# Hybrid encoder step: key caches also laid out token-minor, and attention weights normalised by GpSimd

## The chip, the cores and the metric

The kernel runs on one core of a Trainium2 chip. The metric is device time in microseconds (us) of one execution; three runs of the kernel before are given. The engines are named as the profile names them: PE (TensorE, matrix products and transposes), DVE (VectorE), ACT (ScalarE), POOL (GpSimd), SP (SyncE, which here only issues DMAs).

## The reference

Two layers run over 1024 new frames of one stream (the prompt) and over 16 new frames of each of eight running streams (the samples). The change is in the second layer's attention for the samples. For one sample, with 16 heads and 16 queries each (256 rows), it is

```
def latent_attend(q_lat, q_rope, c, kr, w_uv, mask):
    s = (einsum('bqhk,bsk->bhqs', q_lat, c) + einsum('bqhr,bsr->bhqs', q_rope, kr)) * ATTN_SCALE
    p = softmax(s, axis=-1)
    o_lat = einsum('bhqs,bsk->bqhk', p, c)
    return einsum('bqhk,khv->bqhv', o_lat, w_uv)

c_all  = concatenate([cache_ckv, c_new])      # 1024 past + 16 new rows of 256, per sample
kr_all = concatenate([cache_krope, kr_new])   # the same rows of 64
o = latent_attend(q_lat, q_rope, c_all, kr_all, w_uv, None)
```

The same latent rows `c` are keys (contracted over their 256 features) and values (contracted over the 1040 tokens). The caches arrive token by token, a row of features each.

## The kernel before, in words

The program has five stages, one after the other on the critical engine: mixer A (0 to 583 us of the trace), the middle with the latent keys and the gates (583 to 950), eight head pairs of the prompt's attention (950 to 1573), the eight sample sequences (1573 to about 1726), and the output (to 1943). Each engine's program is written out by hand, and semaphores order them; nothing is scheduled by a planner.

Matrix products are done with both factors split into a rounded high part and a low remainder, three products for each (lines 115 to 117). ACT rounds the high part (`round_high`, line 104), and then DVE subtracts it for the low part (`round_low`, line 109).

For sample i, PE computes `scores(i, 0)` and `scores(i, 1)`, for 128 of the 256 query rows each, and then `values(i - 1)`. Between them it does turns, listed in `TURNS`: W0 to W4 turn the softmax weights `s_p` so that tokens lie on partitions (groups of four 128x128 transposes, W4 of two), and K0 to K6 turn the keys of sequence i + 1 so that features lie on partitions (six groups of four and one of three: 27 transposes for each sequence). The keys of sequence 0 are turned in the last head pair (`turn_first`, from unit `KEYS_FROM` = 9 of its 16 on). Each turned group lands in PSUM; ACT writes its high part (`s_ct_h`, `s_kt_h` for keys, `s_pt_h` for weights), and DVE its low part (`s_ct_l`, `s_kt_l`, `s_pt_l`). Odd and even sequences have their own key buffers.

Softmax on the 128 query rows of one half goes: DVE `largest` (memset of the padding, then the maximum, line 2804), ACT `exp` (line 2669, also sums the rows), DVE `inverted` (reciprocal, line 2808), ACT `normed` (line 2674, scales 128x1056 weights by the reciprocal). `q_low` (line 2737) makes the low parts of the next sequence's queries on DVE, three instructions. SP loads each sequence's cache `s_c_raw`, which is both the values' source and the source of K0 to K3, and the rotary keys `s_kr_raw`.

Of the kernel before, what the change touches and what calls it, by code (L numbers as in the profile page):

```python
# [13 lines left out]
P = 128  # L14
# [988 lines left out]
def middle_programs(nc, k, m, kept_at, heads):  # L1003
# [63 lines left out]
    kvg = late.take("m_kvg", [KVL])  # L1067
    bank = k.bank
# [21 lines left out]
    kv_stored = [m.sem(f"m_kv_stored{i}") for i in range(2)]  # L1090
    (first_high, first_low, wh_ready, wl_ready, gh_ready, gl_ready, y_done, sum_done, stats_done, mv_done, rstd_step,
# [30 lines left out]
    def _(sp):
# [39 lines left out]
        for i in range(NCOL):  # L1162
            if i + 2 < NCOL:
                load_columns(i + 2)
            j = i - 1 - NCQ
            if j >= 0:
                store_gate(j)
                if behind_gate(j)[1] is not None:
                    store_kv(behind_gate(j)[1])
                if j == 8:  # L1170

                    heads.load_first(sp)
                if j == 10:
# [162 lines left out]
    def _(act):  # L1336
# [64 lines left out]
        def turned_high(t):  # L1401
            b, cols = bank[:, 6 + t % 2], slice(t * P, (t + 1) * P)
            act.wait_ge(turned_k, t + 1)
            round_high(nc, k.ct_h[:, :, cols], b[:, 0:2 * P].rearrange("p (a q) -> p a q", a=2))
            round_high(nc, k.kr_h[:, cols], b[:, 2 * P:3 * P]).then_inc(th_k, 1)
# [28 lines left out]
    def _(dve):  # L1434
# [120 lines left out]
        for j in range(HEADS):  # L1555
# [11 lines left out]
            if before is not None:  # L1567
# [7 lines left out]
    def bank_free(pe, b):  # L1575
# [5 lines left out]
        elif b == 6:  # L1581
            pe.wait_ge(c_ready, NT)
# [57 lines left out]
KEYS_FROM = 9  # L1640
NKT = 7
# [16 lines left out]
def heads_programs(nc, k, m, kept_at):  # L1658
# [172 lines left out]
    def _(pe):  # L1831
# [118 lines left out]
        def body(pr, first, last):  # L1950
# [8 lines left out]
            for u in range(UNITS):  # L1959
# [3 lines left out]
                if last and KEYS_FROM <= u < KEYS_FROM + NKT - 1:  # L1963
                    k.samples.turn_first(pe, u - KEYS_FROM)
# [8 lines left out]
            else:  # L1973
                k.samples.turn_first(pe, NKT - 1)
# [313 lines left out]
TURNS = ["W1", "W4", "W2", "W3", "K0", "K1", "K2", "K3", "K4", "K5", "K6", "W0"]  # L2288
BEFORE = TURNS[:4]
# [3 lines left out]
def samples_programs(nc, k, m, kept_at, heads):  # L2293
# [16 lines left out]
    kr_raw = early.take("s_kr_raw", [2, KB + 1, 2, RD])  # L2310
# [9 lines left out]
    block.middle_end = late.regions[0][0]  # L2320
    pt_h, pt_l = late.take("s_pt_h", [KB + 1, QS], F32R), late.take("s_pt_l", [KB + 1, QS], F32R)
# [9 lines left out]
             "o_done o_out ch_ready cl_ready uv_done uv_out og_stored").split()  # L2331
    S = {n: m.sem("s_" + n) for n in names}
    c_loaded = [m.sem(f"s_c_loaded{i}") for i in range(2)]
    kr_loaded = [m.sem(f"s_kr_loaded{i}") for i in range(2)]
    cache_loaded = m.sem("s_cache_loaded")

    def turns(i):

        if not isinstance(i, int):
            return TURNS  # L2340
        return [x for x in TURNS if not (i == 0 and x in BEFORE) and not (i == NSEQ - 1 and x[0] == "K")]

    def turn_number(i, x):

        if isinstance(i, int):
            n = NKT + sum(len(turns(j)) for j in range(i)) + (turns(i).index(x) if i < NSEQ else BEFORE.index(x))
            return n, 6 + n % 2
        at = NKT + len(turns(0)) - len(TURNS) + TURNS.index(x)
        return i * len(TURNS) + at, 6 + at % 2

# [10 lines left out]
    def step_of_keys(j):  # L2361

        return [("c", 0, 0, 4), ("c", 0, 4, 4), ("c", 1, 0, 4), ("c", 1, 4, 4), ("kr", 0, 0, 4), ("kr", 0, 4, 4), ("new", 0, 8, 1)][j]

# [74 lines left out]

    def turn_bank(pe, n, at):  # L2440

        if isinstance(n, int) and n < NKT + 2:
# [4 lines left out]

    def turn_keys(pe, j, b, par):

        what, a, s0, w = step_of_keys(j)  # L2450
        if what == "new":
            for x in range(2):
                nc.tensor.transpose(b[:, x * P:x * P + P], c_raw[par][:, KB, x * P:x * P + P], k.ident[:])
            mm = nc.tensor.transpose(b[:, 2 * P:3 * P], kr_raw[:, par, KB].rearrange("p a b -> p (a b)"), k.ident[:])
        else:
            for x in range(w):
                src = c_raw[par][:, s0 + x, a * P:a * P + P] if what == "c" else kr_raw[:, par, s0 + x].rearrange("p a b -> p (a b)")
                mm = nc.tensor.transpose(b[:, x * P:x * P + P], src, k.ident[:])
        mm.then_inc(S["t_done"], 1)

    def turn_first(pe, j):

        if j == 0:
            heads.bank_free(pe, 1)
            pe.wait_ge(c_loaded[0], 32)
        else:
            pe.wait_ge(S["t_out"], j)
        if j == 4:
            pe.wait_ge(kr_loaded[0], 64)
        turn_keys(pe, j, bank[:, 1], 0)  # L2470

    block.turn_first = turn_first

    @block.tensor
    def _(pe):
# [13 lines left out]
        def turn(x, i, par):  # L2489

            if isinstance(i, int) and i < NSEQ and x not in turns(i):
                return
            n, at = turn_number(i, x)
            if x[0] == "K":

                if x == "K0":
                    pe.wait_ge(c_loaded[1 - par], (i + par) * 16 + 32)
                if x == "K4":
                    pe.wait_ge(kr_loaded[1 - par], (i + par) * 32 + 64)
                turn_keys(pe, int(x[1]), turn_bank(pe, n, at), 1 - par)  # L2500
            else:
                j = int(x[1])
                turn_weights(j, i if j == 0 else i - 1, n, at)

        def scores(i, par, qt, beside):

            q = slice(qt * P, qt * P + P)
            for n, c in enumerate((1, 2, 0) if qt == 0 else (0, 1, 2)):
# [10 lines left out]
                if beside[n]:  # L2519
                    turn(beside[n], i, par)  # L2520

        def values(i, par, beside):


            if isinstance(i, int):
                pe.wait_ge(S["t_out"], turn_number(i + 1, "W3")[0] + 1)
            else:
                pe.wait_ge(S["t_out"], i * len(TURNS) + (turn_number(1, "W3")[0] + 1))
            pe.wait_ge(S["cl_ready"], i * NCP + NCP)
            pe.wait_ge(S["exp_done"], i * 2 + 3 if not (isinstance(i, int) and i == NSEQ - 1) else 2 * NSEQ)  # L2530
            for n in range(6):
# [6 lines left out]
                if beside:  # L2538
                    turn(beside[n], i + 1, 1 - par)

        def body(i, par, first, last):

            pe.wait_ge(S["ql_ready"], i + 1)
            if first:
                for b in range(6):
                    heads.bank_free(pe, b)
                pe.wait_ge(S["t_out"], NKT)
                pe.wait_ge(S["zeroed"], 8)
            else:
                if isinstance(i, int) and i == 1:  # L2550
                    pe.wait_ge(S["zeroed"], 14)
                pe.wait_ge(S["t_out"], turn_number(i, "W1")[0] - 1)

                pe.wait_ge(S["exp_done"], i * 2 - 1)
            if first:

                scores(i, par, 0, ["K0", "K1", "K2"])
                scores(i, par, 1, ["K3", "K4", "K5"])
                for x in ("K6", "W0"):
                    turn(x, i, par)  # L2560
                return
            scores(i, par, 0, ["W1", "W4", "W2"])
# [4 lines left out]
        turn("W1", NSEQ, 0)  # L2567
        k.output.first_columns(pe, 0)
        for x in ("W4", "W2", "W3"):
            turn(x, NSEQ, 0)  # L2570
# [3 lines left out]
        values(NSEQ - 1, 1, None)  # L2574

    def project_values(pe, j):
# [4 lines left out]
        if j < 2:  # L2581
            pe.wait_ge(S["t_out"], turn_number(NSEQ, BEFORE[-1])[0] + 1)
# [50 lines left out]
    def first_keys_high(act, j):  # L2633
        keys_high(act, j, j, 1, 0)
# [627 lines left out]
```

## Time and profile before

| what | value |
|---|---|
| median of three runs | 1944.83 us (1942.0, 1944.83, 1945.01) |
| profiled execution: first to last instruction | 1942.6 us |
| PE busy | 1912.8 us, 98% |
| DVE, ACT, POOL busy | 55%, 39%, 20% |
| first sequence, start to start | 12.84 us |
| a later sequence, start to start | 19.51 to 20.15 us |

The runs list no time apart for the profiled execution; its span lies 2.2 us under the median of the runs. A busy PE means that a product or transpose is in flight. What one sequence costs is read from its start, the first product `ps<-s_ct_h,s_q_l`, to the next sequence's: 1573.30, 1586.14, 1606.29, then every 19.5 to 19.7 us up to 1704.56.

### The profile page before, as it was taken

How to read it: one execution, taken by the hardware profiler on the slowest of the kernel's cores; microseconds unless marked ns; L12 is line 12 of the kernel's file. 1: busy time of each engine (PE TensorE's matmuls, PEld its weight loads, DVE VectorE, ACT ScalarE, POOL GpSimd, SP SyncE). 2: the span in 40 equal slices, each digit the busy share in tenths (PEclk: the TensorE clock that was granted, in tenths of full speed). 3: DMA queues.
4: the chain of work that ended last, by engine and by line, in shares of the span. 5: the costliest groups of instructions: out<-in, count | busy, mean ns of one | idle time of the engine just before them, and what ended most of it. 6: DMA issues, size and time to landing. Idle time of an engine off the chain costs nothing.

```text
span 1942.6 us, 31496 instructions
## 1 busy us (share of the span) xinstructions
PE 1912.8 (98%) x11771; PEld 1807.6 (93%) x11771; DVE 1061.3 (55%) x1943; ACT 767.2 (39%) x1342; POOL 394.0 (20%) x322
## 2 busy tenths in 40 slices
PE   9999999999999999999999999999999999999998
PEld 9999999999987999999999999999999989988886
DVE  4354446445658612332366676666666677653632
ACT  4333233233322222211355555555555567761100
POOL 0221222122311010000042432432433410000000
PEclk9999999999999999999999999999999999999999
DMA  6121122022236312233211112111111253363521
GB/s 183 35 78 54 36 67 78 25 64 68 76 120 201 122 49 70 80 104 106 77 45 50 40 51 64 34 54 54 40 49 42 73 135 93 96 226 136 157 87 44
DMA packets 186082, 158.55 MB, mean 82 GB/s; under 512 B 36144, under 2 KB 170544, under 8 KB 185744
## 3 DMA queue, kind: packets, MB, share of 16 engines
q1 hardware_dynamic: 180784, 139.60, 23.7%
q10 hardware_dynamic: 5040, 17.37, 2.5%
q8 instruction: 58, 0.95, 0.2%
q0 software_dynamic: 176, 0.43, 0.1%
q14 instruction: 24, 0.20, 0.0%
HBM read 115.52 MB, written 41.84 MB: 81 GB/s over the span
## 4 chain that ended last, share of the span: by engine, by line
PE 54%; DVE 7%; issue 5%; ACT 3%; DMA 1%; DVEq 0%; ACTq 0%; SPq 0%
PE ps L115 16%; PE ps L117 16%; PE ps L116 16%; PE ps L1925 1%; PE ps L1908 1%; PE ps L1907 1%; DVE h_pt_l L109 1%; ACT h_p L2042 1%; DVE h_mx L2168 1%; DVE s_mx L2804 1%; DVE h_p L2125 1%; ACT h_p L2031 1%; DVE h_p L2130 1%; DMA m_g_raw<-scratch_o 1%; DVE h_gate L2190 0%
## 5 line engine op out<-in xcount | busy, mean ns | idle before, releaser
L1821 POOL TENSOR_SCALAR h_p<-h_p,h_rsum 128x128 f32<-128x128 f32 (+7 forms) x128 | 220.7, 1726 | 439.8 <-DVE h_rsum L2172 439.8
L115 PE MATMUL ps<-act_h,a_w_l 128*128 128x384 f32 x768 | 270.8, 353 | 1.6 <-DVE a_w_l L109 1.6
L117 PE MATMUL ps<-act_h,a_w_h 128*128 128x384 f32 x768 | 260.1, 339 | 0.0
L116 PE MATMUL ps<-act_l,a_w_h 128*128 128x384 f32 x768 | 259.8, 338 | 0.0
L115 PE MATMUL ps<-act_h,m_c_l 128*128 128x384 f32 x480 | 162.9, 339 | 0.0
L117 PE MATMUL ps<-act_h,m_c_h 128*128 128x384 f32 x480 | 162.6, 339 | 0.0
L116 PE MATMUL ps<-act_l,m_c_h 128*128 128x384 f32 x480 | 162.5, 339 | 0.0
L115 PEld LDWEIGHTS ps<-act_h,a_w_l 128*128 128x128 f32 x768 | 144.2, 188 | 6.4 <-issue 3.3
L116 PEld LDWEIGHTS ps<-act_l,a_w_h 128*128 128x128 f32 x768 | 144.4, 188 | 3.3 <-issue 3.3
L117 PEld LDWEIGHTS ps<-act_h,a_w_h 128*128 128x128 f32 x768 | 144.1, 188 | 0.0
L104 ACT ACTIVATE h_pt_h<-ps 128x128 fp32r<-128x128 f32 (+2 forms) x192 | 86.9, 489 | 106.6 <-PE ps L1925 106.4
L109 DVE TENSOR_TENSOR h_pt_l<-ps,h_pt_h 128x128 fp32r<-128x128 f32 (+2 forms) x192 | 100.2, 550 | 48.1 <-ACT h_pt_h L104 48.1
L2042 ACT ACTIVATE h_p<-ps,h_mx 128x128 f32<-128x128 f32 (+7 forms) x128 | 94.7, 740 | 55.4 <-DVE h_mx L2168 55.0
L115 PE MATMUL ps<-o_w,o_g 128*128 128x512 f32 x288 | 112.4, 390 | 0.8 <-ACT s_olat L2680 0.8
L117 PE MATMUL ps<-o_w,o_g 128*128 128x512 f32 x288 | 112.1, 389 | 0.0
L116 PE MATMUL ps<-o_w,o_g 128*128 128x512 f32 x288 | 112.1, 389 | 0.0
L115 PE MATMUL ps<-cq_h,h_w_l 128*128 128x384 f32 x288 | 102.2, 355 | 0.8 <-DVE h_kt_l L109 0.2
L2168 DVE TENSOR_REDUCE h_mx<-ps 128x1 f32<-128x128 f32 (+7 forms) x128 | 97.0, 758 | 4.4
L117 PE MATMUL ps<-cq_h,h_w_h 128*128 128x384 f32 x288 | 96.6, 335 | 0.0
L116 PE MATMUL ps<-cq_l,h_w_h 128*128 128x384 f32 x288 | 96.5, 335 | 0.0
L115 PE MATMUL ps<-h_pt_h,h_v_l 128*128 128x256 f32 x320 | 88.5, 277 | 4.8 <-DVE h_gate L2190 4.0
L116 PE MATMUL ps<-h_pt_l,h_v_h 128*128 128x256 f32 x320 | 90.1, 282 | 0.0
(320 smaller groups left out, 4817.7 us busy)
## 6 DMA issues: line engine op xcount, KB each, us to landing
a_w_raw<-in_w_in_a SPq DMA_DIRECT2D x31, 512.0 KB, 4.0
m_c_raw<-in_w_in_b SPq DMA_DIRECT2D x20, 512.0 KB, 4.2
scratch_gate<-m_sg SPq DMA_DIRECT2D x16, 576.0 KB, 5.2
o_w_raw<-in_w_out_b SPq DMA_DIRECT2D x16, 512.0 KB, 6.5
h_gate<-scratch_gate SPq DMA_DIRECT2D x62, 128.0 KB, 2.1
scratch_og<-h_gate SPq DMA_DIRECT2D x62, 128.0 KB, 1.7
o_g_raw<-scratch_og SPq DMA_DIRECT2D x24, 256.0 KB, 4.0
a_xn<-in_x SPq DMA_DIRECT2D x9, 512.0 KB, 4.7
```

Source lines behind the costliest of these rows:

```text
L104: return nc.scalar.activation(high, x, ACT.Identity)
L109: return nc.vector.tensor_tensor(low, x, high.bitcast(F32), ALU.subtract)
L115: nc.tensor.matmul(out, ll, rh, start=first, stop=False)
L116: nc.tensor.matmul(out, lh, rl, start=False, stop=False)
L117: return nc.tensor.matmul(out, lh, rh, start=False, stop=last)
L1821: nc.gpsimd.tensor_scalar(weights_of(u), weights_of(u), rsum[:, u % PB], None, ALU.mult).then_inc(S["p_ready"], 1)
L1907: nc.tensor.matmul(out, rq[:, e, q], k.kr_l[:, kc], start=False, stop=False)
L1908: mm = nc.tensor.matmul(out, rq[:, e, q], k.kr_h[:, kc], start=False, stop=True)
L1925: mm = nc.tensor.transpose(bank[:, 4 + i % TB, j * P:j * P + P], p[:, u % PB, key * P:(key + 1) * P], k.ident[:])
L2031: last = nc.scalar.copy(rope_part(tg, 1)[b:b + 32], x[a:a + 32])
L2042: nc.scalar.activation(weights_of(u), scores_of(u), ACT.Exp, bias=mx[:, u % PB], accum_out=rsum[:, u % PB]).then_inc(S["exp_done"], 1)
L2168: nc.vector.tensor_reduce(mx[:, u % PB], scores_of(u), AX.X if n <= BANK else AX.XY, ALU.max, negate=True).then_inc(S["max_done"], 1)
```

## The change

The host gives both caches in a second layout, features on partitions and tokens along the row (`cache_ckv_turned`, `cache_krope_turned`). SP loads them straight into the bytes of the low-part buffers (`s_ct_raw`, `s_kt_raw` are the same memory as `s_ct_l`, `s_kt_l`; sequence 1 has `s_own_raw` for its latent keys). The turns K0 to K6 are gone. Keys are split in three pieces of 128x1040, from SBUF to SBUF, where there were groups of 128x512 from PSUM. The 16 own keys of each sample come through a small DRAM scratch, `scratch_own`, which the middle stage writes: its ninth tile, the samples' tokens, is now turned too (three transposes). In the last head pair the three pieces stand at units 12 and 13 and at the end. The scaling of the weights moves from ACT to POOL (`tensor_scalar`, line 2455 of the changed kernel). PE waits at a sequence's start for all low key parts (`kl_ready`) and the low queries (`ql_ready`).

```diff
-TURNS = ["W1", "W4", "W2", "W3", "K0", "K1", "K2", "K3", "K4", "K5", "K6", "W0"]
-BEFORE = TURNS[:4]
+TURNS = ["W0", "W1", "W4", "W2", "W3"]
+BEFORE = TURNS[1:]
-KEYS_FROM = 9
-NKT = 7
+KEYS_FROM = 12
+NKT = 3
...
+    def load_latent_keys(sp, i, par):
+        raw = latent_raw(i, par)
+        sp.dma_start(raw[:, :, 0:PAST], d["cache_ckv_turned"][bass.ds(i, 1)].rearrange("o p a s -> (o p) a s")).then_inc(ct_loaded[par], 16)
+        sp.dma_start(raw[:, :, PAST:KS], own(i)[:, 0:2]).then_inc(ct_loaded[par], 16)
...
+            sp.wait_ge(S["s_done"], i * 2 - 2)
+            load_latent_keys(sp, i, par)
+            load_rotary_keys(sp, i, par)
             sp.wait_ge(S["cl_ready"], i * NCP - NCP)
-            load(sp, i, par)
-
+            load_cache(sp, i, par)
...
+        def body(i, par, first, last):
+            for qt in range(2):
+                pool.wait_ge(S["inv_done"], i * 2 + qt + 1)
+                pool.sem_inc(S["scale_go"], 1)
+                nc.gpsimd.tensor_scalar(p[:, qt], p[:, qt], rsum[:, qt], None, ALU.mult).then_inc(S["p_ready"], 1)
+        seqs(pool, body)
...
+    def keys_part(i, par, j):
+
+        if j == 2:
+            return kt_raw[par][:, 0:KS], kt_h[par][:, 0:KS], kt_l[par][:, 0:KS]
+        return latent_raw(i, par)[:, j], ct_h[par][:, j, 0:KS], ct_l[par][:, j, 0:KS]
...
+    def keys_low(dve, i, par, j):
+        dve.wait_ge(S["kh_ready"], i * NKT + (j + 1))
+        raw, high, low = keys_part(i, par, j)
+        round_low(nc, low, raw, high).then_inc(S["kl_ready"], 1)
...
             pe.wait_ge(S["ql_ready"], i + 1)
+            pe.wait_ge(S["kl_ready"], i * NKT + NKT)
...
-            scores(i, par, 1, ["W3", "K0", "K1"])
-            values(i - 1, 1 - par, ["K2", "K3", "K4", "K5", "K6", "W0"])
+            scores(i, par, 1, ["W3", None, None])
+            values(i - 1, 1 - par, [None] * 5 + ["W0"])
```

DVE, second half of a sequence, before: the reduction is that of `largest(i, 1)`, `s_pt_l` is a weights' low part, `s_ct_l` and `s_kt_l` are keys of the next sequence, `s_q_l` and `s_rq` its queries; a number behind a name tells buffers apart.

```order
L109 TENSOR_TENSOR s_pt_l<-ps,s_pt_h 128x4x128
L109 TENSOR_TENSOR s_ct_l_3475<-ps,s_ct_h_3474 128x512
L2799 MEMSET ps 128x16
L2804 TENSOR_REDUCE s_mx<-ps 128x1
L109 TENSOR_TENSOR s_ct_l_3475<-ps,s_ct_h_3474 128x512
L2808 RECIPROCAL s_rsum<-s_rsum 128x1
L109 TENSOR_TENSOR s_ct_l_3475<-ps,s_ct_h_3474 128x512 x2
L109 TENSOR_TENSOR s_kt_l_3477<-ps,s_kt_h_3476 128x512
L2737 SCALAR_TENSOR_TENSOR s_q_l<-s_ql_raw,s_q_h 128x256 x2
L2737 SCALAR_TENSOR_TENSOR s_rq<-s_qr_raw,s_rq 64x256
```

And of the change, at the same place:

```order
L109 TENSOR_TENSOR s_pt_l<-ps,s_pt_h 128x4x128
L109 TENSOR_TENSOR s_ct_l_3476<-s_ct_raw_3492,s_ct_h_3475 128x1040
L2745 MEMSET ps 128x16
L2750 TENSOR_REDUCE s_mx<-ps 128x1
L109 TENSOR_TENSOR s_ct_l_3476<-s_ct_raw_3492,s_ct_h_3475 128x1040
L2754 RECIPROCAL s_rsum<-s_rsum 128x1
L109 TENSOR_TENSOR s_kt_l_3478<-s_kt_raw_3494,s_kt_h_3477 128x1040
L2695 SCALAR_TENSOR_TENSOR s_q_l<-s_ql_raw,s_q_h 128x256 x2
L2695 SCALAR_TENSOR_TENSOR s_rq<-s_qr_raw,s_rq 64x256
```

Seven key pieces have become three longer ones; the first stands between the last weights' low part and the maximum of the second half, the last between the reciprocal and the queries, and both inputs of each now lie in SBUF.

ACT at the same place, before: line 2669 is `exp`, line 2674 is `normed`, line 2603 the queries' high part.

```order
L104 ACTIVATE s_pt_h<-ps 128x4x128
L2674 ACTIVATE s_p<-s_p,s_rsum 128x1056
L104 ACTIVATE s_ct_h_3474<-ps 128x512 x2
L2669 ACTIVATE s_p,s_rsum<-ps,s_mx 128x1056
L104 ACTIVATE s_ct_h_3474<-ps 128x512
L2674 ACTIVATE s_p<-s_p,s_rsum 128x1056
L104 ACTIVATE s_ct_h_3474<-ps 128x512
L104 ACTIVATE s_kt_h_3476<-ps 128x512
L2603 ACTIVATE s_q_h<-s_ql_raw 128x256 x2
```

And of the change:

```order
L104 ACTIVATE s_pt_h<-ps 128x4x128
L104 ACTIVATE s_ct_h_3475<-s_ct_raw_3492 128x1040
L2641 ACTIVATE s_p,s_rsum<-ps,s_mx 128x1056
L104 ACTIVATE s_ct_h_3475<-s_ct_raw_3492 128x1040
L104 ACTIVATE s_kt_h_3477<-s_kt_raw_3494 128x1040
L2575 ACTIVATE s_q_h<-s_ql_raw 128x256 x2
```

Both scalings are gone from ACT, and the first key piece follows the last weights' high part directly.

DVE late in the last head pair, before: `h_mx` is the maximum of a 128x1024 tile of prompt scores, `h_gate` the gated result that frees a bank for PE.

```order
L2172 RECIPROCAL h_rsum<-h_rsum 128x1
L109 TENSOR_TENSOR s_ct_l_3475<-ps,s_ct_h_3474 128x512
L2164 MEMSET ps 64x64
L2168 TENSOR_REDUCE h_mx<-ps 128x1
L2190 TENSOR_TENSOR h_gate<-ps,h_gate 128x256
L109 TENSOR_TENSOR h_pt_l_3429<-ps,h_pt_h_3427 128x3x128
L109 TENSOR_TENSOR s_kt_l_3477<-ps,s_kt_h_3476 128x512
L2172 RECIPROCAL h_rsum<-h_rsum 128x1
```

And of the change:

```order
L2177 RECIPROCAL h_rsum<-h_rsum 128x1
L109 TENSOR_TENSOR s_ct_l_3476<-s_ct_raw_3492,s_ct_h_3475 128x1040
L2169 MEMSET ps 64x64
L2173 TENSOR_REDUCE h_mx<-ps 128x1
L2195 TENSOR_TENSOR h_gate<-ps,h_gate 128x256
L109 TENSOR_TENSOR h_pt_l_3429<-ps,h_pt_h_3427 128x3x128
L109 TENSOR_TENSOR s_ct_l_3476<-s_ct_raw_3492,s_ct_h_3475 128x1040
L2177 RECIPROCAL h_rsum<-h_rsum 128x1
```

The order of the places is the same, with a piece of 1040 columns in each where one of 512 stood.

## Rows read from the trace of the kernel before

**Rows 1.** Windows by sequence: length, busy (count) by engine, PEclk, DMA, GB/s.
```profile
1573.30:1586.14 12.84, 11.42 (x81) 10.87 (x81) 9.44 (x19) 7.15 (x13) 0.78 (x6) 1.00 0.52 137
1586.14:1606.29 20.15, 19.65 (x150) 18.88 (x149) 14.06 (x26) 15.55 (x31) 0.00 (x0) 1.00 0.00 1
1606.29:1625.99 19.70, 19.34 (x148) 18.89 (x148) 14.09 (x25) 14.37 (x28) 0.00 (x0) 1.00 0.33 82
...
1685.05:1704.56 19.51, 19.28 (x148) 18.88 (x148) 14.08 (x25) 14.43 (x29) 0.00 (x0) 1.00 0.58 157
```

**Rows 2.** Timeline of PE, four turns among values: start, length, instruction.
```profile
1597.27 0.28 PE L117 MATMUL ps<-s_pt_h,s_c_h 128*128 128x256 f32 x1
1597.39 0.60 PE L2458 MATMUL ps<-ident,h_w_raw 128*128 128x128 f32 x4
...
1597.95 0.28 PE L116 MATMUL ps<-s_pt_l,s_c_h 128*128 128x256 f32 x1
```

**Rows 3.** Groups by line and shape: count, busy us, mean ns.
```profile
L104 ACT ACTIVATE o_w<-o_w_raw 128x1024 fp32r<-128x1024 f32 x16 | 16.0, 1054 | 19.6 <-DMA o_w_raw<-in_w_out_b 19.6
...
L109 DVE TENSOR_TENSOR o_w<-o_w_raw,o_w 128x1024 fp32r<-128x1024 f32 x16 | 18.9, 1220 | 8.4 <-ACT o_w L104 8.4
...
L1821 POOL TENSOR_SCALAR h_p<-h_p,h_rsum 128x1024 f32<-128x1024 f32 x16 | 45.5, 2847 | 48.7 <-DVE h_rsum L2172 48.7
```

**Rows 4.** Timeline of ACT in the sequence that starts at 1606.29.
```profile
1614.23 1.18 ACT L2674 ACTIVATE s_p<-s_p,s_rsum 128x1056 f32<-128x1056 f32 x1
...
1618.02 1.14 ACT L2669 ACTIVATE s_p<-ps,s_mx 128x1056 f32<-128x1056 f32 x1 [0.75 <-DVE s_mx L2804]
...
1619.15 0.59 ACT L104 ACTIVATE s_ct_h<-ps 128x512 fp32r<-128x512 f32 x1
```

**Rows 5.** Timeline of DVE in the same sequence.
```profile
1613.89 0.16 DVE L2808 RECIPROCAL s_rsum<-s_rsum 128x1 f32<-128x1 f32 x1 [0.70 <-ACT s_p L2669]
...
1622.89 0.76 DVE L2737 SCALAR_TENSOR_TENSOR s_q_l<-s_ql_raw,s_q_h 128x256 fp32r<-128x256 f32 x2 [0.28 <-ACT s_rq L2604]
1623.67 0.42 DVE L2737 SCALAR_TENSOR_TENSOR s_rq<-s_qr_raw,s_rq 64x256 fp32r<-64x256 f32 x1
```

**Rows 6.** Timeline of DVE and PE at the start of the next sequence.
```profile
1625.69 0.16 DVE L109 TENSOR_TENSOR s_kt_l<-ps,s_kt_h 128x16 fp32r<-128x16 f32 x1
...
1625.99 0.42 PE L115 MATMUL ps<-s_ct_h,s_q_l 128*128 128x352 f32 x1 [0.35 <-DVE s_kt_l L109]
```

**Rows 7.** Timeline of POOL and DVE in an earlier head pair.
```profile
1006.29 1.90 POOL L1821 TENSOR_SCALAR h_p<-h_p,h_rsum 128x640 f32<-128x640 f32 x1 [2.66 <-DVE h_rsum L2172]
...
1006.58 1.65 DVE L109 TENSOR_TENSOR h_w_l<-h_w_raw,h_w_h 128x512 fp32r<-128x512 f32 x2
1008.16 1.27 DVE L109 TENSOR_TENSOR h_pt_l<-ps,h_pt_h 128x512 fp32r<-128x512 f32 x2
```

**Rows 8.** Instructions of lines 964 and 756: shortest/median/longest ns, first and last start.
```profile
L964 DVE TENSOR_TENSOR a_decay_b<-a_decay x8: 311/2520/2523, 63.6 to 528.8; 128x8 f32<-128x8 f32 x8
...
L756 POOL TENSOR_TENSOR a_kin<-a_kin,a_kk x8: 2676/2678/3191, 63.5 to 529.1; 128x1152 f32<-128x1152 f32 x8
```

**Rows 9.** Timeline of PE at two idle stretches, and a window's granted clock.
```profile
593.77 1.04 PE L1235 MATMUL ps<-ident,m_x 128*128 128x128 f32 x8
...
597.33 0.77 PE L115 MATMUL ps<-m_w_h,m_g_l 128*128 128x512 f32 x1 [2.52 <-DVE m_x L1456]
...
597.30:600.70 3.40, 3.37 (x8) 2.75 (x9) 3.32 (x7) 1.95 (x2) 1.06 (x2) 0.50 1.06 327
...
1585.73 0.66 PE L2483 MATMUL ps<-ident,s_p 128*128 128x128 f32 x4 [1.42 <-DVE s_kt_l L109]
```

**Rows 10.** Timeline of DVE and PE late in the last head pair.
```profile
1559.83 0.67 DVE L109 TENSOR_TENSOR s_ct_l<-ps,s_ct_h 128x512 fp32r<-128x512 f32 x1
...
1560.65 1.22 DVE L2168 TENSOR_REDUCE h_mx<-ps 128x1 f32<-128x1024 f32 x1
...
1562.35 0.36 PE L115 MATMUL ps<-h_pt_h,h_v_l 128*128 128x256 f32 x1 [1.14 <-DVE h_gate L2190]
```

More of the change, by code:

```diff
@@ L1067, in middle_programs @@
     kvg = late.take("m_kvg", [KVL])
+    own = late.take("m_own", [3 * P])
     bank = k.bank
@@ L1403, in turned_high @@
             act.wait_ge(turned_k, t + 1)
+            if t == NT - 1:
+                nc.scalar.copy(own[:], b[:, 0:3 * P]).then_inc(th_k, 1)
+                return
             round_high(nc, k.ct_h[:, :, cols], b[:, 0:2 * P].rearrange("p (a q) -> p a q", a=2))
@@ L1566, in _ @@
             before, now = behind_gate(j)
-            if before is not None:
+            if before is not None and before < NPB:
                 turned_low_latent(before)
@@ L2330, in samples_programs, with turn_number @@
     names = ("q_loaded uv_loaded zeroed qh_ready ql_ready s_done masked max_done exp_done inv_done p_ready t_done t_high t_out "
-             "o_done o_out ch_ready cl_ready uv_done uv_out og_stored").split()
+             "o_done o_out ch_ready cl_ready kh_ready kl_ready uv_done uv_out og_stored scale_go").split()
     S = {n: m.sem("s_" + n) for n in names}
     c_loaded = [m.sem(f"s_c_loaded{i}") for i in range(2)]
[L2334 to L2349, printed above, removed]
+    ct_loaded = [m.sem(f"s_ct_loaded{i}") for i in range(2)]
+    kt_loaded = [m.sem(f"s_kt_loaded{i}") for i in range(2)]
+    def turn_number(i, x, par):
+        at = TURNS.index(x)
+        return i * len(TURNS) + at, 6 + (par + at) % 2
     def seqs(eng, body):
@@ L2446, in turn_bank @@
         return bank[:, at]
[L2448 to L2472, printed above, removed]
     @block.tensor
@@ L2489, in turn @@
         def turn(x, i, par):
[L2491 to L2503, printed above, removed]
+            n, at = turn_number(i, x, par)
+            turn_weights(int(x[1]), i, n, at)
         def scores(i, par, qt, beside):
@@ L2519, in scores @@
                 if beside[n]:
-                    turn(beside[n], i, par)
+                    turn(beside[n], i - 1, 1 - par)
         def values(i, par, beside):
[L2525 to L2528, printed above, removed]
+            pe.wait_ge(S["t_out"], i * len(TURNS) + len(TURNS))
             pe.wait_ge(S["cl_ready"], i * NCP + NCP)
@@ L2546, in body @@
                     heads.bank_free(pe, b)
[L2547 to L2560, printed above, removed]
+                pe.wait_ge(S["zeroed"], 6)
+                for qt in range(2):
+                    scores(i, par, qt, [None] * 3)
+                turn("W0", i, par)
                 return
+            if isinstance(i, int) and i == 1:
+                pe.wait_ge(S["zeroed"], 12)
+            pe.wait_ge(S["exp_done"], i * 2 - 1)
             scores(i, par, 0, ["W1", "W4", "W2"])
             pe.wait_ge(S["exp_done"], i * 2)
-            scores(i, par, 1, ["W3", "K0", "K1"])
-            values(i - 1, 1 - par, ["K2", "K3", "K4", "K5", "K6", "W0"])
+            scores(i, par, 1, ["W3", None, None])
+            values(i - 1, 1 - par, [None] * 5 + ["W0"])
         seqs(pe, body)
-        turn("W1", NSEQ, 0)
+        turn("W1", NSEQ - 1, 1)
         k.output.first_columns(pe, 0)
         for x in ("W4", "W2", "W3"):
-            turn(x, NSEQ, 0)
+            turn(x, NSEQ - 1, 1)
         k.output.first_columns(pe, 1)
         pe.wait_ge(S["o_out"], NSEQ - 1)
-        values(NSEQ - 1, 1, None)
+        values(NSEQ - 1, 1, [None] * 6)
     def project_values(pe, j):
```

187 lines of the change are left out of this document (78 added, 109 removed).

## The prediction

> **What bounds the kernel now.** I read the page first (PE busy nearly throughout, in all five stages), then windows of the sample stage, cut at each sequence's first product, then the timelines of PE, DVE and ACT inside one sequence, and last what POOL does elsewhere. The windows are to show that a later sequence takes 19.70 us of which PE is busy 19.34 [rows 1]: PE is the bound of this stage, and DVE and ACT, busy 14 us each, are not. So the first question is how much PE work goes; the second, whether what DVE and ACT must do in sequence now fits under what is left.
>
> **What the turns of keys cost.** Four turns among the values stand between the product at 1597.27 and the one at 1597.95 [rows 2]. Products of that width follow each other by 0.12 (1597.27 to the turns at 1597.39), so these 0.68 us hold two steps of 0.12 and 0.44 of turns. Six groups of 0.44 and one of three at an estimated 0.33 make 2.97 us a sequence. The start of a sequence also loses 0.35 to the key piece that ends last [rows 6]. Without both, PE by itself needs 19.70 - 2.97 - 0.35 = about 16.4 us.
>
> **What DVE and ACT need.** I follow the new order from a sequence's start (1606.29 in the trace) and put each new piece where its engine is free. The stretch ahead of it does not change: ACT is done with the last weights at 1614.23, 7.94 after the start, where the scaling began [rows 4].
> - Keys high, 128x1040 from SBUF: 1054 ns for 1024 columns [rows 3], so 1.07: ACT until 9.01.
> - Keys low, two SBUF inputs: 1220 ns for 1024 columns [rows 3], so 1.24: DVE from 9.04 to 10.28. Then the maximum, 0.15 behind the piece's end (1559.83 + 0.67 against 1560.65) and 1.22 for 1024 columns [rows 10], 1.26 here: it ends at 11.69.
> - Exp from 11.72; the next ACT instruction stands 1.13 behind its start [rows 4]: the second keys high from 12.85 to 13.92, the third behind it to 15.0, the queries' high part behind that.
> - Second keys low from 13.95, the reciprocal at 15.12 (a DVE instruction starts some 0.07 before the one ahead of it is recorded as ended: 1.27 for two of 0.67 [rows 7]), third keys low from 15.2 to 16.4.
> - The queries' low part: 1622.89 to 1623.67 + 0.42, 1.20 us [rows 5]: until 17.57. PE starts 0.14 after its last releaser (1625.69 + 0.16 to 1625.99 [rows 6]): **17.7 us**.
>
> So the chain on DVE and ACT takes the bound over: 17.7 where PE would need 16.4. It is one loop: PE's start releases the scores, they release maximum and exp, and the keys and queries behind them release PE's next start. What is late next is that start, every time. Before, seven smaller pieces were woven between the waits and did not lie in one line.
>
> **The scaling on POOL.** 2847 ns for 1024 columns [rows 3], 2.94 for 1056, against ACT's 1.18 [rows 4]. ACT's two slots of 1.18 are freed. For the first half POOL starts some 0.2 after the reciprocal at 1613.89, at 7.9, and ends at 10.9; the turns that read those weights come when the values are over, behind 13: hidden. For the second half it is later than the reciprocal at 15.2, by the third keys low; its readers (W4, W2, W3) stand in the next sequence's scores, from 2.6 us after their start: hidden up to an end at 21. If a scaling were later than that, W4's wait on PE would be the price.
>
> What is not hidden is the meeting of POOL with DVE where DVE reads two tiles in SBUF. The trace has one such meeting with the very instruction: POOL's scaling of 640 columns starts at 1006.29, and two DVE pieces of 512 that start at 1006.58 take 1.65 together, where two take 1.27 alone [rows 7]; so one is held 0.38, until 0.66 after POOL's start, a third of POOL's 1.90. There are seven such pairs and all look alike. Here the first scaling starts at 7.9 and the first keys low at 9.04, 1.1 behind it: 0.66 scaled by columns is 1.09, so it is just let through. The second scaling is asked for at 15.3, while the third keys low runs (15.2 to 16.4); it gets its turn then, and the queries' low part, also with two SBUF inputs, starts in the same moment. It is held for a time r. Bounds: nothing, if this three-operand form does not meet POOL; 0.66 or 1.09, by the row as it is or by columns; 2.94, if POOL keeps the way for its whole length, as the row of line 964 can be read (a 0.31 us instruction takes 2.52 beside POOL's 2.68 in line 756 [rows 8]; there POOL reads two tiles). I take 0.9, between the readings of the row with the same POOL instruction. The period is then **18.6 us**, with 2.2 us of waiting on PE.
>
> The Trainium skill ("SBUF — State Buffer", "Who interferes with whom") says that the port pair which DVE and GpSimd share is an exclusive lock held for a whole instruction, and that a DVE instruction with two SBUF inputs meets a GpSimd one that reads SBUF. By it r is POOL's whole length and the sum is the first rival's; the row at 1006 shows DVE held for a third of it only.
>
> **The sum**, against the profiled span of 1942.6 (2.2 under the median of the runs):
> - Six periods from the second sequence's start at 1586.14 to the last one's at 1704.56 take 118.42 [rows 1]; 6 x 18.6 = 111.6: **-6.8**.
> - The first sequence has no values: 12.84 [rows 1]. Its turns of keys go from PE, and its end is set by W0, which waits for POOL: 24 products of 0.16 bring the first half's scores at 4.0, maximum and exp bring the weights at 6.7, the reciprocal and its hop 7.2, POOL 2.94, W0 0.4; the third keys low, at 10.7, is as late. About 10.9: **-1.9**.
> - The middle gets three transposes and a copy: **+0.3** (three quarters of 0.44), the DMA of them lies under the gates that are still to come.
> - The last head pair loses 3 us of turns on PE, but PE waits there already, 1.14 at 1562.35 for the gated result behind a maximum at 1560.65 that stands behind a keys low of 0.67 [rows 10]. A piece of 1.24, whose high part takes 1.07 where a piece of 512 took 0.59 [rows 4], sends that maximum 0.8 later, and the next piece of the same length delays the last reciprocal by 0.6 more; the lighter PE gives most of it back. **+0.5**, between -1.9 and +2.
> - The last sequence and the output: DVE there holds weights' pieces with two SBUF inputs against POOL, covered by PE's first output columns: **0**, up to +1.
>
> Together -7.9: **1937 us** against 1944.83.
>
> **The rivals.**
> - *POOL keeps DVE off for its whole length* (slower). The first keys low at 9.04 waits for the scaling that ends at 10.9, 1.86 more, and the queries 2.94: 17.7 + 4.8 = 22.5 a period, six of them 135, +16.6; with the other terms about 1960. Row of line 964 for it, the seven pairs at 1006 against it. It decides from a holding of about 2.0 us a period on: there 17.7 + 2.0 reaches the old 19.7. Chance 0.13.
> - *PE's clock falls at each wait* (no change). At 597.33 PE had been idle 2.52 after 1.04 of transposes, 3.5 us without a product, and the granted clock for the next 3.4 us was 0.50, the 1.2 GHz level [rows 9]. At that level products follow by twice the time, some 1.5 us lost at each fall. After 1.42 idle at 1585.73 [rows 9] the clock stayed at 1.00 through the second sequence [rows 1]. The new wait of 2.2 with W0's turns ahead of it (0.4) lies between the two, nearer to the lower. Six falls cost 9: 1945. Chance 0.20. The Trainium skill ("TensorE: Matmul & The Clock Gate", Part 1) also has the clock set by how busy PE has been of late; by it a wait in every sequence may cost more than its length, which is this rival.
> - *No holding at all* (faster still). r = 0, period 17.7, six periods 106.2, -12.2; with the last pair at its even value 1931, with the last pair at its best 1929. For it: the queries' form is not the one seen held. Chance 0.17.
> - That the change would not do what it says, leaving PE the bound at 16.4, needs the chain above to be wrong by a whole piece; I give it nothing of its own.
>
> **How the numbers follow.** Main case 0.50, at 1937; its own range is 1933 to 1941. Taken with the rivals but the first, the range is from 1928.5 (no holding, best last pair) to 1947 (falls of the clock and a last pair at +2): it leaves out the first rival and a little else, under 2 in 10. A measurement here can tell 0.2%, 3.9 us: faster is below 1940.9, slower above 1948.7. Faster: 0.45 of the main case, 0.17 of the third, some of the second: 0.66. Same: 0.05 of the main case, most of the second: 0.20. Slower: the first, and a little of the second: 0.14.
>
> **What would show it.** Windows cut at the sequences' starts should be 18.6 long with PE busy 16.4; PE should wait about 2 us at each start, released by DVE's `s_rq`, where it waited 0.35 for `s_kt_l`. The queries' low part should be recorded about 0.9 longer than 0.76, and POOL's second scaling should start late or be longer than 2.94. The granted clock should stay at 1.00. In the first sequence W0 should wait for POOL's `s_p`, and in the last pair the wait of 1.14 should have grown. If the first keys low is recorded at 3 us, the first rival has it; if a window shows a clock of 0.50 after each start, the second. The prediction is wrong as well if W4's turns wait for POOL, or if the turned caches land after the keys' slot on ACT.

## The result

The changed kernel takes 1945.84 us (median of 20 runs, 1943.58 to 1949.79); the kernel before, in as many runs, 1942.52. The ratio is 1.0014, 95% interval 1.0007 to 1.0020: 0.14% slower, less than the 0.2% that the prediction took as what a measurement can tell. Forecast was a gain of 8 us; the time measured lies near the upper end of the stated range, where the second rival stood. The profiled execution (1942.0 us span, a time of 1943.75) is the second fastest of the 20.

### The profile page after: what moved, and what is told of

It reads as the page before. It is cut to its first block, busy times and chain, and to the rows that moved or that the text cites. A ratio compares the mean times of both kernels' runs of the same rounds, so it can differ in the third digit from the quotient of the medians.

```text
span 1942.0 us, 30962 instructions
## 1 busy us (share of the span) xinstructions
PE 1896.3 (98%) x11558; PEld 1792.3 (92%) x11558; DVE 1061.8 (55%) x1903; ACT 745.2 (38%) x1287; POOL 450.6 (23%) x336
## 4 chain that ended last, share of the span: by engine, by line
PE 52%; DVE 7%; issue 5%; ACT 3%; DMA 2%; SPq 1%; DVEq 0%; POOL 0%; ACTq 0%; POOLq 0%
PE ps L115 16%; PE ps L117 15%; PE ps L116 15%; PE ps L1934 1%; PE ps L1917 1%; PE ps L1916 1%; DVE h_pt_l L109 1%; DVE s_mx L2750 1%; ACT h_p L2047 1%; DVE h_mx L2173 1%; DVE h_p L2130 1%; ACT s_ct_h L104 1%; ACT h_p L2036 1%; DMA s_qr_raw<-scratch_qr 1%; DVE h_p L2135 1%
```

## The profile after

Windows of the changed kernel, cut at the sequences' first products as in [rows 1]:

```profile
1570.97:1582.88 11.91, 8.46 (x55) 8.20 (x54) 10.45 (x16) 6.80 (x11) 4.44 (x8) 0.99 0.56 161
1582.88:1602.77 19.89, 17.80 (x122) 17.36 (x121) 13.57 (x20) 12.86 (x22) 8.32 (x3) 0.92 0.62 187
1602.77:1623.01 20.24, 17.98 (x120) 17.55 (x121) 14.15 (x21) 11.53 (x20) 6.98 (x3) 0.92 0.45 132
1623.01:1643.27 20.26, 18.00 (x121) 17.57 (x121) 14.21 (x21) 11.53 (x20) 6.98 (x3) 0.92 0.44 132
1683.56:1703.44 19.88, 17.96 (x120) 17.42 (x120) 14.24 (x21) 11.53 (x20) 6.97 (x3) 0.91 0.38 121
```

The first period is 0.9 shorter than before, the next six together are 120.6 where they were 118.4. PE has lost its turns of keys (121 instructions for 148), yet a period is 20.2, and the column of the granted clock, 1.00 before, reads 0.92 and 0.91.

Timeline of PE at a sequence's start; it answers to [rows 6]:

```profile
1620.15 0.60 PE L2475 MATMUL ps<-ident,s_p 128*128 128x128 f32 x4
1623.01 0.43 PE L115 MATMUL ps<-s_ct_h,s_q_l 128*128 128x352 f32 x1 [2.26 <-DVE s_rq L2695]
1623.28 0.32 PE L116 MATMUL ps<-s_ct_l,s_q_h 128*128 128x352 f32 x1
1623.44 0.45 PE L117 MATMUL ps<-s_ct_h,s_q_h 128*128 128x352 f32 x1
...
1624.27 0.50 PE L117 MATMUL ps<-s_ct_h,s_q_h 128*128 128x352 f32 x1
1624.56 0.50 PE L2496 MATMUL ps<-s_kt_l,s_rq 128*128 128x352 f32 x1
1624.85 0.50 PE L2497 MATMUL ps<-s_kt_h,s_rq 128*128 128x352 f32 x1
```

PE waits 2.26 for the queries' low part. Two products later the step from one to the next goes from 0.16 to 0.29. Windows of that stretch show why:

```profile
1620.50:1623.50 3.00, 0.74 (x6) 0.50 (x5) 2.96 (x5) 2.19 (x5) 3.00 (x1) 1.00 0.12 19
1623.50:1626.90 3.40, 3.40 (x15) 3.33 (x14) 1.77 (x4) 0.66 (x2) 0.40 (x1) 0.50 0.56 164
1626.90:1643.20 16.30, 14.11 (x106) 13.73 (x105) 11.88 (x18) 10.87 (x19) 6.03 (x2) 1.00 0.43 130
```

For 3.4 us the clock is at 0.50, the 1.2 GHz level, and then at full speed up to the next start. The trace has this once near the start of each of sequences 1 to 6, at 1582.5, 1603.0, 1623.5, 1644.0, 1664.4 and 1684.9, behind waits of 3.45 (for W0) and 2.08 to 2.26; not in sequence 7, behind one of 1.93. The falls do not keep their place: the first begins 0.4 ahead of its sequence's start, the sixth 1.4 behind it. Half the work of 3.4 us is 1.7 us each.

DVE in the same period, the keys' low parts and the queries' (it answers to [rows 5]):

```profile
1633.74 1.24 DVE L109 TENSOR_TENSOR s_ct_l<-s_ct_raw,s_ct_h 128x1040 fp32r<-128x1040 f32 x1 [0.27 <-ACT s_ct_h L104]
...
1639.85 1.22 DVE L109 TENSOR_TENSOR s_kt_l<-s_kt_raw,s_kt_h 128x1040 fp32r<-128x1040 f32 x1
1640.99 1.62 DVE L2695 SCALAR_TENSOR_TENSOR s_q_l<-s_ql_raw,s_q_h 128x256 fp32r<-128x256 f32 x2
1642.62 0.42 DVE L2695 SCALAR_TENSOR_TENSOR s_rq<-s_qr_raw,s_rq 64x256 fp32r<-64x256 f32 x1
```

And POOL's two scalings there:

```profile
1632.66 2.96 POOL L2455 TENSOR_SCALAR s_p<-s_p,s_rsum 128x1056 f32<-128x1056 f32 x1 [8.76 <-DVE s_rsum L2754]
1640.13 4.02 POOL L2455 TENSOR_SCALAR s_p<-s_p,s_rsum 128x1056 f32<-128x1056 f32 x1 [4.51 <-DVE s_rsum L2754]
```

The first keys low starts 1.08 behind POOL's first scaling and takes its own 1.24; it is not held. The two queries' instructions take 1.62 where they took 0.76, and POOL's second scaling, asked for while the third keys low runs, is recorded at 4.02 instead of 2.96.

The first sequence, on ACT, DVE, POOL and PE:

```profile
1573.68 2.04 ACT L104 ACTIVATE s_ct_h<-s_own_raw 128x1040 fp32r<-128x1040 f32 x2 [1.37 <-DMA s_own_raw<-scratch_own]
...
1574.95 1.23 DVE L109 TENSOR_TENSOR s_ct_l<-s_own_raw,s_ct_h 128x1040 fp32r<-128x1040 f32 x1
...
1576.29 1.26 DVE L2750 TENSOR_REDUCE s_mx<-ps 128x1 f32<-128x1056 f32 x1
...
1579.21 5.90 POOL L2455 TENSOR_SCALAR s_p<-s_p,s_rsum 128x1056 f32<-128x1056 f32 x2 [5.37 <-DVE s_rsum L2754]
...
1582.32 0.91 PE L2475 MATMUL ps<-ident,s_p 128*128 128x128 f32 x4 [3.45 <-POOL s_p L2455]
```

The keys of sequence 1 are late by a DMA (1.37), their low part stands ahead of the first maximum on DVE, and W0 waits 3.45 for POOL. In the last head pair, DVE and PE (it answers to [rows 10]):

```profile
1557.27 1.24 DVE L109 TENSOR_TENSOR s_ct_l<-s_ct_raw,s_ct_h 128x1040 fp32r<-128x1040 f32 x1
...
1558.66 1.22 DVE L2173 TENSOR_REDUCE h_mx<-ps 128x1 f32<-128x1024 f32 x1
...
1560.36 0.35 PE L115 MATMUL ps<-h_pt_h,h_v_l 128*128 128x256 f32 x1 [3.07 <-DVE h_gate L2195]
```

The longer keys low is ahead of the last maximum, and PE's wait is 3.07 where it was 1.14.

## The experiments

After the forecast had failed, theory one was: the chain on DVE and ACT takes the 18.6 of the forecast, and the clock's fall behind each wait costs the rest. Its rival: the chain itself is 20.2 long, and the clock falls where PE has nothing to do anyway. The times are medians, and each ratio is to the kernel before on the same chip (1942.88 to 1943.43 there). All windows and rows are of one profiled execution each.

**Filling the wait** (`fill`).

```diff
+FILL = 22
+FILL_FIRST = 34
...
+        def fill(n):
+            for _ in range(n):
+                nc.tensor.transpose(bank[:, 1, 3 * P:4 * P], k.ident[:], k.ident[:])
...
+            if not first:
+                pe.wait_ge(S["exp_done"], i * 2 - 1)
+                fill(FILL)
             pe.wait_ge(S["ql_ready"], i + 1)
...
+                pe.wait_ge(S["exp_done"], 1)
+                fill(FILL_FIRST)
                 turn("W0", i, par)
```

> The changed kernel with 22 transposes of the identity on PE, into a free bank, ahead of the wait at the start of sequences 1 to 7, and 34 ahead of W0 in sequence 0; nothing else. Theory one (the clock gives the gain back: the chain on DVE and ACT takes 18.6 us, and the stretch at 1.2 GHz behind each wait costs some 1.65 more): granted clock 1.00 throughout the samples, six periods of 18.6 to 18.8 instead of 20.2, in all 10 to 12 us under the changed kernel, about 1934. Rival (the chain itself takes 20.2, the clock only falls where PE would wait anyway): periods stay at 20.1 to 20.3, the time within 2 us of the changed kernel.

1940.37 us, ratio 0.9979 (0.9970 to 0.9989). Windows of two sequences:

```profile
1626.22:1644.86 18.64, 18.64 (x145) 18.40 (x143) 14.17 (x21) 11.55 (x20) 6.99 (x3) 1.00 0.49 144
1644.86:1663.49 18.63, 18.63 (x145) 18.38 (x143) 14.16 (x21) 11.54 (x20) 6.99 (x3) 1.00 0.49 143
```

18.64 and 18.63, the clock at 1.00, with work that nobody uses: theory one, and the forecast's 18.6. All six periods take 111.55 (1589.01 to 1700.56); the forecast had 111.6, the changed kernel took 120.56. The total fell less than expected, by 5.5 instead of 10 to 12 against the changed kernel. In the trace the 34 transposes of sequence 0 began only at 1582.55 and made its period 14.19 instead of 11.91; two falls, at 597.7 and at 1563.7, are not in the changed kernel's profiled execution.

**Filling half of it** (`fill10`): the same with `FILL = 10` and none in sequence 0.

> The changed kernel with 10 transposes of the identity ahead of the wait at the start of sequences 1 to 7 (22 before), none in sequence 0. The wait left on PE is about 1.2 us of 2.2. Theory one, the length of the stretch without work decides whether the clock falls: no falls, six periods of 18.6, the one in the first sequence stays; about 9 us under the changed kernel, 1937. Rival, any wait for DVE at a start brings the fall: periods 20.2, time as the changed kernel, 1946.

1937.51 us, ratio 0.9969 (0.9958 to 0.9981), as expected. A start on PE, and windows of one period and of the stretch behind the wait in sequence 0:

```profile
1626.13 0.40 PE L115 MATMUL ps<-s_ct_h,s_q_l 128*128 128x352 f32 x1 [1.19 <-DVE s_rq L2703]
```

```profile
1626.13:1644.82 18.69, 17.50 (x131) 17.14 (x131) 14.17 (x21) 11.53 (x20) 6.99 (x3) 1.00 0.48 142
1587.10:1590.50 3.40, 3.40 (x15) 3.33 (x14) 1.65 (x2) 0.81 (x2) 1.61 (x1) 0.50 1.07 268
```

A wait of 1.19 stays, and the clock does not fall; behind the wait of 3.46 in sequence 0, where nothing was filled, it does. So a wait for DVE alone doesn't bring it: here those of 2.2 did, and those of 1.2 did not.

**The reciprocal behind the queries** (`late_recip`).

```diff
-            inverted(i, 1)
             if not last:
                 keys_low(dve, i + 1, 1 - par, 2)
                 q_low(dve, i + 1, 1 - par)
+            inverted(i, 1)
```

> The changed kernel with the second half's reciprocal on DVE behind the queries' low part, so that POOL's scaling cannot meet it. If POOL holds DVE for 0.9: the queries' low part is recorded at 0.76 again, the chain ends at 17.7, the wait at the start is 1.2 to 1.4; POOL's weights come about 0.6 late for W4, period 18.2 to 18.4 and no fall of the clock, in all about 11 us under the changed kernel, 1935; with falls all the same, 1945. If the 0.9 has another cause (the queries' high part on ACT, say): the low part stays at 1.62, and periods are over 20.

1937.32 us, ratio 0.9962 (0.9948 to 0.9976). DVE, PE and the window of one period:

```profile
1641.38 0.76 DVE L2695 SCALAR_TENSOR_TENSOR s_q_l<-s_ql_raw,s_q_h 128x256 fp32r<-128x256 f32 x2
1642.16 0.42 DVE L2695 SCALAR_TENSOR_TENSOR s_rq<-s_qr_raw,s_rq 64x256 fp32r<-64x256 f32 x1
1642.61 0.16 DVE L2754 RECIPROCAL s_rsum<-s_rsum 128x1 f32<-128x1 f32 x1
```

```profile
1642.81 0.42 PE L115 MATMUL ps<-s_ct_h,s_q_l 128*128 128x352 f32 x1 [1.32 <-DVE s_rq L2695]
...
1646.51 0.39 PE L2478 MATMUL ps<-ident,s_p 128*16 128x128 f32 x2 [0.46 <-POOL s_p L2455]
```

```profile
1624.46:1642.81 18.35, 16.60 (x121) 15.98 (x121) 13.74 (x21) 11.54 (x21) 6.44 (x2) 1.00 0.48 146
```

The queries' low part is back at 0.76, the wait at 1.32, W4 waits 0.46 for POOL, and the clock stays up in these periods. The 0.86 was POOL's holding; it lengthened the wait from 1.3 to 2.2, and the fall came with that. The total fell by 8.5 where 11 was expected; this execution has falls at 598.0 and 1563.9 and one of 6.8 us at 1584.4, behind W0's wait.

**All keys high ahead of exp** (`early`). In the changed kernel ACT sits idle 2.7 us there:

```profile
1636.39 1.14 ACT L2641 ACTIVATE s_p<-ps,s_mx 128x1056 f32<-128x1056 f32 x1 [2.68 <-DVE s_mx L2750]
```

```diff
-                keys_high(act, i + 1, 1 - par, 0)
+                for j in range(NKT):
+                    keys_high(act, i + 1, 1 - par, j)
             exp(i, 1)
             if not last:
-                keys_high(act, i + 1, 1 - par, 1)
-            if not last:
-                keys_high(act, i + 1, 1 - par, 2)
                 q_high(act, i + 1, 1 - par)
```

> The changed kernel with all three keys high on ACT ahead of exp of the second half, where ACT sits idle 2.7 us; DVE's order as it is. Theory one: the keys and queries are ready about 15.5 to 16.4 us after a start, PE is the bound again at 16.4 to 16.8 a period, hardly a wait, no fall of the clock: six periods near 99 where they took 121, in all about 20 us under the changed kernel, 1925. Rival (another wait of the sequence, such as W4 for POOL's weights or the results, takes the place): a wait of 1 us or more stays on PE in each period, the clock still falls, and the time is above 1935.

1925.59 us, ratio 0.9912 (0.9895 to 0.9928). ACT in one period, and windows of two:

```profile
1641.83 2.04 ACT L104 ACTIVATE s_ct_h<-s_ct_raw 128x1040 fp32r<-128x1040 f32 x2
1643.75 1.07 ACT L104 ACTIVATE s_kt_h<-s_kt_raw 128x1040 fp32r<-128x1040 f32 x1
1645.58 1.15 ACT L2641 ACTIVATE s_p<-ps,s_mx 128x1056 f32<-128x1056 f32 x1 [0.75 <-DVE s_mx L2748]
```

```profile
1617.15:1633.80 16.65, 16.39 (x121) 16.01 (x121) 14.36 (x21) 11.75 (x22) 7.10 (x3) 1.00 0.54 161
1633.80:1650.38 16.58, 16.39 (x121) 15.99 (x121) 14.23 (x21) 11.61 (x21) 6.96 (x3) 1.00 0.53 160
```

PE is the bound again at 16.6, as its own need of 16.4 had it: the three pieces are done before the maximum that exp waits for, which still holds it up by 0.75. The six periods take 98.77 (1584.23 to 1683.00) where the kernel before took 118.42, 3.3 a period less. This is the gain that the removed turns are worth.

**The scaling back on ACT** (`act_norm`), behind W3's high part and behind the second keys high; POOL's loop is taken out.

```diff
             high("W3", i - 1, 1 - par)
+            normed(i, 0)
...
                 keys_high(act, i + 1, 1 - par, 1)
+            normed(i, 1)
             if not last:
                 keys_high(act, i + 1, 1 - par, 2)
```

> The changed kernel with the scaling back on ACT, behind W3's high part and behind the second keys high. Theory one: no DVE instruction is held (queries' low part 0.76 again, -0.9), but each scaling puts 1.1 into the chain ahead of a key piece: chain 18.9 to 19.7, and the clock falls as before, periods 20.6 to 21.4, total 2 to 7 us over the changed kernel. Rival (the holding of DVE by POOL is the main loss): periods about 19.3, total 5 us under the changed kernel.

1964.39 us, ratio 1.0106 (1.0089 to 1.0123), a miss for both. ACT and a start on PE:

```profile
1672.38 1.18 ACT L2639 ACTIVATE s_p<-s_p,s_rsum 128x1056 f32<-128x1056 f32 x1 [1.38 <-DVE s_rsum L2755]
1673.46 1.05 ACT L104 ACTIVATE s_kt_h<-s_kt_raw 128x1040 fp32r<-128x1040 f32 x1
```

```profile
1653.45 0.66 PE L115 MATMUL ps<-s_ct_h,s_q_l 128*128 128x352 f32 x1 [4.78 <-DVE s_rq L2696]
```

I had priced the scaling as 1.1 of ACT's time. But it waits 1.38 for a reciprocal that stands behind the second keys low on DVE, and the third keys high waits behind it. PE's wait is 4.78, and the clock is at 0.50 for 6.8 us, from 1652.1, within the wait, to 1659.0. The queries' low part takes its own 0.75:

```profile
1675.70 0.75 DVE L2696 SCALAR_TENSOR_TENSOR s_q_l<-s_ql_raw,s_q_h 128x256 fp32r<-128x256 f32 x2
```

So without POOL there is no holding here either. With this order of ACT and DVE, the move to POOL is what keeps the new keys from costing more.

**The scaling on POOL alone** (`pool_only`): the kernel before with its two `normed` calls on ACT taken out and POOL's loop put in.

> The kernel before with the scaling on POOL alone; keys are still turned on PE. Theory one: PE stays the bound, the clock stays at 1.00, DVE's queries are held 0.9 where the K5 and K6 pieces stand behind them, so periods 19.7 to 20.5 and W0 of the first sequence about 1 to 2 us later: total +1 to +7 over the kernel before. Rival (POOL's 2.9 us put a wait into the turns of weights): a wait for POOL's weights on PE in every sequence, clock falls, +10 or more.

1944.39 us, ratio 1.0004 (0.9995 to 1.0014): no change. A window of one period:

```profile
1626.11:1645.82 19.71, 19.34 (x148) 18.91 (x148) 14.19 (x25) 12.53 (x26) 5.93 (x2) 1.00 0.33 82
```

19.71, as before: PE stays the bound and hides it. The moved scaling by itself shows neither a cost nor a gain (+1.1, at the low end of the +1 to +7 expected).

**The ends of the sample stage.** Four versions of `early` put sequence 0's key pieces at other units of the last head pair, or its two scalings on ACT with its first maximum ahead of the keys. The first is `early_pair`:

```diff
-KEYS_FROM = 12
+KEYS_FROM = 13
```

> The kernel with all keys high early, and with the first sequence's key pieces one unit later in the last head pair (units 13 and 14 and the end), so that none stands ahead of the last maximum. Theory: the wait of 3.08 on PE in the last pair shrinks to about 1 or 2, and the fall of the clock that follows it in some executions goes; 1.5 to 3 us under that kernel, about 1923. Rival: the pieces pushed later make the samples' first start wait for the keys' low parts, and nothing is gained.

1924.79 us, 0.9901 (0.9884 to 0.9917), level with `early` within the intervals. PE's wait in the pair fell from 3.08 to 1.70, though this execution has a fall of the clock at 1568.4 all the same; ACT and PE at the stage's start show the next limit:

```profile
1570.56 0.72 ACT L2575 ACTIVATE s_q_h<-s_ql_raw 128x256 fp32r<-128x256 f32 x2 [4.73 <-DMA s_qr_raw<-scratch_qr]
...
1574.34 0.40 PE L115 MATMUL ps<-s_ct_h,s_q_l 128*128 128x352 f32 x1 [1.48 <-issue]
```

The queries' load holds ACT 4.73, and PE starts no earlier. The key pieces were not it: the expected rival had the place, not the cause. `early_pair_first`, on top of it:

```diff
-            for qt in range(2):
+            for qt in range(0 if first else 2):
                 pool.wait_ge(S["inv_done"], i * 2 + qt + 1)
...
                 exp(i, 0)
+                normed(i, 0)
                 keys_high(act, i + 1, 1 - par, 2)
                 exp(i, 1)
+                normed(i, 1)
...
-                keys_low(dve, i + 1, 1 - par, 0)
                 largest(i, 0)
+                keys_low(dve, i + 1, 1 - par, 0)
+                inverted(i, 0)
                 keys_low(dve, i + 1, 1 - par, 1)
-                inverted(i, 0)
                 largest(i, 1)
```

> The kernel of the run before this one, with sequence 0's two scalings on ACT, which is idle there, and its first maximum ahead of the next sequence's keys on DVE. Theory: W0 of sequence 0 no longer waits 3.3 for POOL; a wait of about 2 for the last keys' low part is left, the first period 10.8 instead of 11.6, in all 1 to 2.5 us under the run before this one. Rival: W4 or the exp of the second half waits longer instead, and nothing is gained.

1924.29 us, 0.9902 (0.9885 to 0.9918). The first period is 10.76, as expected, and the wait of 3.5 for W0 is down to 0.45; against the run before it the total cannot be told apart (1 to 2.5 us were expected). The same at the change's own units (`early_first`):

> All keys high early and sequence 0's scalings on ACT, with the key pieces of sequence 0 where the change has them in the last head pair (units 12, 13 and the end). If the wait of 1.2 to 1.5 at the samples' first start came from the pieces put one unit later, it is gone here; the wait of 3.1 in the last pair is back, with a fall of the clock in some executions. About 1 us under or level with the kernel that has them later: 1923 to 1924.5.

1923.71 us, 0.9901 (0.9884 to 0.9917): no wait at the first start, the one of 3.08 in the pair back with a fall of the clock at 1561.6. With `KEY_UNITS = (11, 13)` (`early_first_units`):

> The same with the two pieces at units 11 and 13. If the last maximum is what PE's wait of 3.1 hangs on, a piece less ahead of it shortens that wait by 1.2 or more, and the first start does not wait: about 1 us under the same kernel with units 12 and 13. If the piece at unit 11 only delays the exp and the reciprocal there, the wait moves to an earlier unit and nothing is gained.

1924.15 us, 0.9907 (0.9890 to 0.9923). Its wait in the pair is 1.85, not 3.08, yet a fall of the clock follows at 1561.3 all the same, and its first start has a wait of 1.04 in exchange, behind 2.10 of ACT's for the queries' load: nothing is gained. All four lie within each other's intervals; the lowest median is 1923.71, some 20 us (1%) under both kernels.

## Why the prediction was wrong

It named the waits and the mechanism, and put them on the wrong side of the clock. Forecast was -7.9; the medians moved by +3.3 (1942.52 to 1945.84; the three runs that the forecast started from had 2.3 more). Most of the 11.2 between them lies in the six periods. By its steps:

- **PE's own need, 16.4.** Right: `early` runs at 16.6 with PE busy 16.39.
- **The chain on DVE and ACT, 17.7, and with POOL's holding 18.6.** Right: 18.63 in `fill`, where nothing else was in the way. The estimate of 0.9 for the holding measured 0.86, and the wait of 2.2 measured 2.26. Without the holding, `late_recip` has a period of 18.35, of which 0.46 is W4's wait for POOL: 17.9.
- **That the clock would stay at 1.00 behind a wait of 2.2.** This is the step that failed. The prediction put the wait with W0's turns ahead of it "nearer to the lower" of two cases and gave the fall 0.20. Its own rows put it nearer to the upper: with the turns 2.6, against 3.5 counted the same way and 1.42; without them 2.2, against 2.52 and 1.42. The fall came at six of the seven starts behind a wait. It made periods of 20.24 to 20.26 where `fill` has 18.63 to 18.68, and over the six cost 9.0 (120.56 against 111.55), 1.5 each: the second rival's price. Its 1945 should read 1946 by its own terms (1937 and 9); 1945.84 was measured.
- **Six periods, -6.8.** +2.1 instead (120.56 against 118.42): 8.9 of the miss.
- **The first sequence, -1.9.** -0.9: the wait of keys for their DMA and the keys low ahead of the first maximum put the first exp at 1577.58, 6.6 behind the start, where I had it over by 6.7; W0 came at 11.35 instead of 10.2.
- **The middle, +0.3.** From the middle's first product `m_c_h` to the heads' first `h_kt_l` it is 309.93 after (657.81 to 967.74) and 309.60 before: +0.33.
- **The last pair, +0.5.** -0.6 in the profiled execution (heads' first product to the samples' first, 603.23 against 603.84), with the wait of 3.07 in it and no fall behind it. Other executions of the same stretch have one: at 1563.7 in `fill`, 1561.8 in `early`, 1563.4 in `act_norm`, each behind a wait of 3.1. The changed kernel's median is 2.1 over its profiled run. Runs near the median have a mean granted clock of 0.992 or 0.993, the profiled one 0.994, and a fall takes 0.0009 off it (half of 3.4 us in 1942): one or two falls more. Where they lie no trace shows, so that they are in this pair is argued.
- **The last sequence and the output, 0.** +0.5 (238.56 from the last start to the end, against 238.04).
- **What the spans owe to chance.** The two profiled spans differ by -0.6, not by +3.3. Up to the first product with `m_c_h` the changed kernel's is 2.05 shorter (657.81 against 659.86), and 1.6 of that is the fall at 597.3 that this execution of it does not have.
- **The first rival, POOL holding DVE for its whole length.** Wrong by the rows: the queries' low part was held for 0.86 of a scaling of 2.96, and a keys low that starts 1.08 behind POOL is not held at all. The Trainium skill's rule ("SBUF — State Buffer", "Who interferes with whom") is borne out in that the two meet (0.76 became 1.62, and 0.76 again once POOL's turn was moved), and not in that the lock lasts a whole instruction.

The gain of the change is there: 27 transposes and the wait behind them a sequence, 3.3 us, as `early` has it. It was spent in two halves: the key work, now in three long pieces, stood in line behind exp and ahead of the queries, so PE waited 2.2 for it; and six of those waits, the first of them W0's, were followed by a stretch at half clock, 1.5 each. Moving two ACT instructions ahead of exp brings it back.

## What to carry to other kernels

A wait on PE is not priced by its length alone: where the clock fell behind it (at the starts here, behind 2.1 to 2.3 us, not behind 0.8 to 1.3), it cost 1.5 more, and six small waits can eat a gain that was worked out correctly. When work is taken off the bound engine, follow what its helpers then do in sequence, and put what has no need of a result ahead of the wait for it. A cheap test tells such a loss from the chain itself: give the idle engine useless work, and see whether the kernel gets faster.

## What the runs showed that was not expected

- The same wait does not always bring the fall. The wait of 2.5 at 597 in the middle was followed by 0.50 before [rows 9], in `fill` (597.7), in `fill10` (597.2) and in `late_recip` (598.0), but not in the changed kernel's profiled execution, where it was 2.46; that of 3.07 in its last pair was followed by none either. And in `early_pair` one came at 1568.4 behind waits of 1.11, 0.94 and 0.61 within five us, none of them long, while `early_pair_first` has the same three waits and no fall. In the samples it came behind every wait of 2.08 or more but one: W0's of 3.31 in sequence 0 of `early`, which ends at 1583.85, was followed by 1.00, the like ones of 3.20 to 3.46 in the changed kernel, `fill10`, `late_recip` and `early_pair` by 0.50. So the length of a wait alone does not decide it; what else does was not tried.
- The clock stayed at 0.50 for 3.4 us behind most waits, for 6.8 behind those of 4.6 to 4.8 in `act_norm` and behind one of 3.2 in `late_recip`.
- Runs of the changed kernel spread over 6.2 us (1943.58 to 1949.79), with a mean granted clock of 0.993 in the shortest and 0.990 in the longest; those of the kernel before over 4.1.
- POOL's scaling holds a DVE instruction with two SBUF inputs for about 0.9 of its 2.96 us, counted from when POOL itself gets through.
